# One fused kernel of two transformer blocks: high parts of split products first, the first loads on two queues, other step orders

## What is computed

```
layer 0: x = LN(a*x + mlstm(x))         mlstm: x @ w_in (3080 columns), 4 heads, gates, head norm, @ w_out
         x = LN(a*x + relu(x @ up)^2 @ down)      up: 1024 x 4096, down: 4096 x 1024
         x = x + sigmoid(x @ w_gate + b) * (p[0] @ w_proj)
layer 1: x = LN(a*x + attention with sinks and a window (x)), then the same two lines
block 2: h = h + 0.5 * (silu(n(h) @ wg) * (n(h) @ wu)) @ wd        n = rmsnorm, width 2816
         h = h + mixed(n(h)) @ w_out    mixed: compressed, selected and window attention, and one with forget gates
         h = h + 0.5 * swiglu again
         h = h + sigmoid(n(h) @ w_gate) * n(p @ w_proj)
```

## Time and profile before

| | |
|---|---|
| median of 3 runs | 1231.56 us (1231.07 to 1232.04) |
| profiled execution | 1232.38 us, its span 1230.7 us |
| TensorE (PE) busy | 1198.8 us, 97%, 5861 matmuls |
| weight loads (PEld) | 991.3 us, 81% |
| VectorE (DVE) | 745.4 us, 61% |
| ScalarE (ACT) | 618.3 us, 50% |
| GpSimd (POOL) | 43.2 us, 4% |
| memory traffic | 210.72 MB, mean 171 GB/s |

### The profile page before, as it was taken

How to read it: one execution, slowest core, us unless ns; L and a number is a source line. 1 busy time by engine, 2 the same in 40 slices (tenths; PEclk the granted TensorE clock), 3 DMA queues, 4 the chain that set the end, 5 groups by cost and what they waited for, 6 DMA issues and landing times.

```text
span 1230.7 us, 15102 instructions
## 1 busy us (share of the span) xinstructions
PE 1198.8 (97%) x5861; PEld 991.3 (81%) x5861; DVE 745.4 (61%) x983; ACT 618.3 (50%) x925; POOL 43.2 (4%) x61
## 2 busy tenths in 40 slices
PE   7999999999999989999999999999999999999998
PEld 6887788888788768888877888888878788888877
DVE  5648754545876585455587545447976465545456
ACT  4554434434465544434446444436886565444445
POOL 1000000000000000000000000000202010000001
PEclk9999999999999999999999999999999999999999
DMA  8546455465652454655545555564652327555550
GB/s 285 183 150 221 154 206 184 160 207 188 201 180 76 138 196 163 204 190 173 189 151 184 192 181 172 195 206 128 189 172 69 112 75 235 187 181 176 191 171 35
DMA packets 119959, 210.72 MB, mean 171 GB/s; under 512 B 8320, under 2 KB 67024, under 8 KB 119888
## 3 DMA queue, kind: packets, MB, share of 16 engines
q1 hardware_dynamic: 119888, 209.75, 51.5%
HBM read 208.68 MB, written 1.05 MB: 170 GB/s over the span
## 4 chain that ended last, share of the span: by engine, by line
PE 89%; DVE 7%; ACT 1%; issue 1%; DMA 1%; POOL 0%; SPq 0%; DVEq 0%; POOLq 0%; ACTq 0%
PE psum L341 26%; PE psum L343 26%; PE psum L342 26%; PE psum L1333 2%; PE psum L1365 2%; PE psum L480 2%; DVE wl L324 1%; PE psum L1352 1%; PE psum L787 1%; DVE xT_low L742 1%; DVE bn L709 1%; DMA ring<-in_a_w_in 1%; PE psum L1336 0%; DVE x L733 0%; ACT xT_high L765 0%
## 5 line engine op out<-in xcount | busy, mean ns | idle before, releaser
L293 DVE TENSOR_TENSOR wl<-ring,wh 128x2048 fp32r<-128x2048 f32 x131 | 300.0, 2292 | 270.5 <-ACT wh L284 270.5
L341 PE MATMUL psum<-wh,xT_high 128*128 128x512 f32 (+4 forms) x944 | 371.6, 394 | 3.3 <-DVE xT_low L3414 1.9
L343 PE MATMUL psum<-wh,xT_low 128*128 128x512 f32 (+4 forms) x944 | 362.8, 384 | 0.0
L342 PE MATMUL psum<-wl,xT_high 128*128 128x512 f32 (+4 forms) x944 | 362.0, 383 | 0.0
L284 ACT ACTIVATE wh<-ring 128x2048 fp32r<-128x2048 f32 x131 | 250.5, 1915 | 218.9 <-PE psum L343 218.9
L341 PEld LDWEIGHTS psum<-wh,xT_high 128*128 128x128 f32 x944 | 178.2, 189 | 36.6 <-DVE wl L324 2.3
L343 PEld LDWEIGHTS psum<-wh,xT_low 128*128 128x128 f32 x944 | 177.9, 188 | 34.9
L342 PEld LDWEIGHTS psum<-wl,xT_high 128*128 128x128 f32 x944 | 178.4, 189 | 31.1
L341 PE MATMUL psum<-wh,hidT_high 128*128 128x512 f32 (+1 forms) x520 | 199.5, 385 | 2.6 <-DVE hidT_low L3506 1.9
L343 PE MATMUL psum<-wh,hidT_low 128*128 128x512 f32 (+1 forms) x520 | 197.3, 381 | 0.0
L342 PE MATMUL psum<-wl,hidT_high 128*128 128x512 f32 (+1 forms) x520 | 197.2, 381 | 0.0
(11 more groups left out here) (289 smaller groups left out, 1080.0 us busy)
## 6 DMA issues: line engine op xcount, KB each, us to landing
ring<-in_mlp_w_up SPq DMA_DIRECT2D x32, 1024.0 KB, 5.3
ring<-in_mlp_w_down SPq DMA_DIRECT2D x32, 1024.0 KB, 4.9
ring<-in_ffn_wg SPq DMA_DIRECT2D x44, 512.0 KB, 4.0
ring<-in_ffn_wu SPq DMA_DIRECT2D x44, 512.0 KB, 5.0
ring<-in_ffn_wd SPq DMA_DIRECT2D x22, 1024.0 KB, 5.1
ring<-in_ple_w_gate SPq DMA_DIRECT2D x12, 1024.0 KB, 5.2
ring<-in_w_in SPq DMA_DIRECT2D x10, 1024.0 KB, 5.1
ring<-in_a_w_in SPq DMA_DIRECT2D x8, 1024.0 KB, 9.8
```

The source lines that it names most:

```text
L293: K.nc.vector.tensor_tensor(low[:, 0:w], K.ring[:, n % SLOTS, 0:w], high[:, 0:w].bitcast(F32), ALU.subtract).then_inc(K.low_ready, 2)
L341: nc.tensor.matmul(out, x[0], w[0], start=start, stop=False)
L342: nc.tensor.matmul(out, x[0], w[1], start=False, stop=False)
L343: return nc.tensor.matmul(out, x[1], w[0], start=False, stop=stop)
```

## The change

Five things are done.

1. `product` is taken apart into `product_high` (the two matmuls with x high) and `product_low` (the one with x low). `up_half_turned` makes a half of a product behind a turn: it waits for `high`, makes 8 matmuls, waits for `low`, makes 4. It is used for every `lead` and for t = 1 of the first product of each stage behind a tail (also in `dense` of the sink and the last mixer, written out there, and in `embed`). The waits are now per half, not for all four.
2. `step`, `piece` and `last` of the output products make the high matmuls first and wait for `z_low` in the middle; the wait ahead of them is for `z_high`.
3. `lead` of a feed-forward writes bank 0, and the readers of that bank follow through `up_bank`.
4. At the start the first half of load 0 is issued by ScalarE; SyncE issues the first half of `x`, the second half of load 0, the second half of `x`. The first `dense` steps take k = 0 and 1 and are placed before `xturn` 2 and 3, and they wait per pair for `input_high` and `input_low`.
5. The step lists of the first mixer, the sinks mixer and all nine tails are in another order.

```diff
+def product_high(K, out, x, w, start):
+    nc = K.nc
+    nc.tensor.matmul(out, x[0], w[0], start=start, stop=False)
+    nc.tensor.matmul(out, x[0], w[1], start=False, stop=False)
+
+def product_low(K, out, x, w, stop):
+    return K.nc.tensor.matmul(out, x[1], w[0], start=False, stop=stop)
...
+def up_half_turned(K, pe, where, gated, n, half, t, high, low):
...
+    pe.wait_ge(K.high_turned.sem, high)
+    for k in range(KT // 2):
+        if gated and k == 0 or not gated and k % 2 == 0:
+            weights_here(K, pe, n, 1 if gated else k // 2)
+        product_high(K, out, xs(k), [x[:, k, :, :] for x in w], half == 0 and k == 0)
+    pe.wait_ge(K.low_turned.sem, low)
+    for k in range(KT // 2):
+        mm = product_low(K, out, xs(k), [x[:, k, :, :] for x in w], half == 1 and k == KT // 2 - 1)
     return mm
...
+    up_bank = lambda c, t: 0 if led and c == 0 and t == 0 else 4 + t
...
-            if c == 0:
-                pe.wait_ge(K.low_turned.sem, x_low0)
...
+                if c == 0:
+                    mm = up_half_turned(K, pe, up_bank(c, t), gated, n, half, t, x_high0 - 1 + half, x_low0 - 1 + half)
...
             elif step == "lead":
                 half, = args
                 where, gated = self.lead
-                pe.wait_ge(K.low_turned.sem, self.low0 + half + 1)
                 if own and half == 0:
                     own("free")
-                mm = up_half(K, pe, where, gated, self.lead_load + half, half, 0)
+                mm = up_half_turned(K, pe, where, gated, self.lead_load + half, half, 0, self.high0 + half + 1,
+                                    self.low0 + half + 1)
...
-    def last(self, pe, load, t, h):
+    def last(self, pe, load, t, h, low=None):
...
+            product_high(K, K.psum[:, 2 * t + h, :], self.stat(2 * load + k, t), w[k], False)
+        if low:
+            pe.wait_ge(K.z_low.sem, low)
+        for k in range(2):
+            mm = product_low(K, K.psum[:, 2 * t + h, :], self.stat(2 * load + k, t), w[k], load == 3 and k == 1)
...
-        to_ffn, to_gated, to_rest = (4, False), (4, True), (0, False)
+        to_ffn, to_gated, to_rest = (0, False), (0, True), (0, False)
```

The start, in the first mixer's list, on SyncE and on ScalarE:

```diff
+        yield "xturn", 0
+        yield "xturn", 1
         yield "high", 0, 0
         yield "low", 0, 0
+        yield "dense", 0, 0, 0, range(2)
+        yield "dense", 0, 0, 1, range(2)
+        yield "high", 0, 1
         yield "low", 0, 1
-        yield "high", 0, 1
-        yield "xturn", 0
-        yield "xturn", 1
         yield "xturn", 2
         yield "xturn", 3
+        yield "dense", 0, 0, 0, range(2, 4)
+        yield "dense", 0, 0, 1, range(2, 4)
...
-        for half, x_sem, w_sem in ((0, K.input_loaded, K.first_loaded), (1, K.rest_loaded, K.slot_loaded[0])):
...
+        sp.dma_start(K.x[:, :, 0:BANK], x_rows[:, :, 0:BANK]).then_inc(K.input_loaded, 16)
+        for dst, src in zip(pieces_in(K, 0, K.ring[:, 0, :]), K.loads[0]):
+            sp.dma_start(dst[:, 2:4, :], src[:, 2:4, :]).then_inc(K.slot_loaded[0], 16)
+        sp.dma_start(K.x[:, :, BANK:D], x_rows[:, :, BANK:D]).then_inc(K.rest_loaded, 16)
...
+        for dst, src in zip(pieces_in(K, 0, K.ring[:, 0, :]), K.loads[0]):
+            act.dma_start(dst[:, 0:2, :], src[:, 0:2, :]).then_inc(K.first_loaded, 16)
```

More of the change, by code:

```diff
@@ L852, in after_mlstm @@
     yield "normal", 0, 1
+    yield "low", 0, 0
+    yield "last", 3, 1
     yield "turn", 0, 1
-    yield "last", 3, 1
     yield "lead", 0
@@ L1213, in after_ffn2 @@
     yield "emb", 1, 1
+    yield "copy", 0, 0
+    yield "square", 0, 1
+    yield "copy", 0, 1
+    yield "lead_high", 1, 1
     yield "high", 0, 1
[L1215 removed]
     yield "copy", 1, 0
     yield "copy", 1, 1
[L1218 to L1219 removed]
+    yield "high", 1, 0
     yield "lead_low", 1, 0
+    yield "low", 0, 1
+    yield "turn", 1, 0
+    yield "turn", 1, 1
+    yield "lead", 0
     yield "lead_low", 1, 1
[L1222 to L1224 removed]
     yield "low", 1, 0
     yield "low", 1, 1
[L1227 removed]
     yield "square", 1, 0
+    yield "high", 1, 1
     yield "square", 1, 1
[L1230 removed]
     yield "lead", 1
@@ L1626, in steps @@
         yield "high", 2, 0
-        yield "dense", 0, 0, 1, range(2)
+        yield "dense", 0, 0, 1, range(4)
         yield "high", 2, 1
         yield "low", 2, 0
-        yield "take", 0, 0
         yield "high", 3, 0
         yield "low", 2, 1
-        yield "dense", 0, 0, 1, range(2, 4)
-        yield "low", 3, 0
-        yield "high", 3, 1
         yield "dense", 0, 1, 1, range(2)
         yield "dense", 0, 1, 1, range(2, 4)
+        yield "take", 0, 0
         yield "take", 0, 1
+        yield "high", 3, 1
@@ L1639, in steps @@
         yield "high", 4, 0
         yield "rotate", 0
-        yield "low", 3, 1
         yield "dense", 1, 0, 0, range(2)
         yield "dense", 1, 0, 0, range(2, 4)
+        yield "high", 4, 1
+        yield "low", 3, 0
+        yield "dense", 1, 0, 1, range(2)
+        yield "tiles", 0
+        yield "dense", 1, 0, 1, range(2, 4)
+        yield "low", 3, 1
+        yield "tiles", 2
+        yield "tiles", 1
         yield "residual", 0
-        yield "dense", 1, 0, 1, range(2)
-        yield "high", 4, 1
+        yield "dense", 1, 1, 0, range(2)
@@ L1661, in steps @@
         yield "scores", 2
+        yield "low", 5, 0
+        yield "dense", 1, 1, 1, range(2, 4)
+        yield "high", 6, 0
+        yield "take", 1, 1
+        yield "scores", 3
         yield "turn", 0
-        yield "low", 5, 0
+        yield "dense", 2, 0, 0, range(2)
         yield "low", 5, 1
-        yield "dense", 1, 1, 1, range(2, 4)
-        yield "take", 1, 1
-        yield "dense", 2, 0, 0, range(2)
+        yield "dense", 2, 0, 0, range(2, 4)
+        yield "high", 6, 1
+        yield "rotate", 1
@@ L1683, in steps @@
-        yield "dense", 2, 0, 1, range(2, 4)
-        yield "low", 6, 0
-        yield "values", 2
-        yield "high", 7, 0
+        yield "turn", 3
+        yield "values", 2
+        yield "dense", 2, 0, 1, range(2, 4)
+        yield "high", 7, 0
+        yield "high", 7, 1
+        yield "low", 6, 0
+        yield "values", 3
+        yield "shares", 0
+        yield "dense", 2, 1, 0, range(2)
+        yield "group", 0
+        yield "low", 6, 1
         yield "scores", 5
-        yield "low", 6, 1
@@ L1689, in steps @@
-        yield "high", 7, 1
-        yield "values", 3
         yield "turn", 4
-        yield "group", 0
-        yield "dense", 2, 1, 0, range(2)
         yield "scores", 6
-        yield "turn", 5
-        yield "dense", 2, 1, 0, range(2, 4)
-        yield "take", 2, 0
-        yield "scores", 7
-        yield "sink", 1
         yield "low", 7, 0
         yield "low", 7, 1
+        yield "dense", 2, 1, 0, range(2, 4)
+        yield "turn", 5
+        yield "zturn", 0
+        yield "scores", 7
@@ L1731, in steps @@
         yield "scores", 11
-        yield "turn", 10
+        yield "low", 8, 1
         yield "values", 8
@@ L2617, in own @@
                 if load == 2 and h == 0:
-                    pe.wait_ge(K.z_low.sem, zl0 + 4)
-                out.last(pe, load, 1, h)
+                    pe.wait_ge(K.z_high.sem, zh0 + 4)
+                out.last(pe, load, 1, h, zl0 + 4)
         follow.pe(pe, own)
@@ L3012, in steps @@
         yield "take", 1, 1
+        yield "colturn",
+        yield "low", 5, 1
         yield "high", 6, 1
         yield "tiles", 0
+        yield "gcol",
         yield "tiles", 1
-        yield "gcol",
-        yield "take", 2, 0
-        yield "dense", 2, 1, 0, range(4)
-        yield "tiles", 2
-        yield "high", 7, 0
-        yield "high", 7, 1
-        yield "dense", 2, 1, 1, range(4)
+        yield "high", 7, 0
+        yield "low", 6, 0
+        yield "dense", 2, 1, 0, range(4)
+        yield "low", 6, 1
@@ L3023, in steps @@
+        yield "tiles", 2
+        yield "high", 7, 1
+        yield "angle",
+        yield "dense", 2, 1, 1, range(4)
+        yield "scores", 0
+        yield "take", 2, 0
+        yield "dense", 3, 0, 0, range(4)
+        yield "low", 7, 0
         yield "high", 8, 0
-        yield "low", 6, 1
-        yield "low", 7, 0
         yield "take", 2, 1
-        yield "angle",
-        yield "scores", 0
-        yield "dense", 3, 0, 0, range(4)
+        yield "low", 7, 1
+        yield "dense", 3, 0, 1, range(4)
@@ L3030, in steps @@
         yield "high", 8, 1
-        yield "dense", 3, 0, 1, range(4)
-        yield "low", 7, 1
+        yield "high", 9, 0
+        yield "low", 8, 0
         yield "tiles", 3
-        yield "high", 9, 0
+        yield "low", 8, 1
         yield "high", 9, 1
         yield "scores", 1
-        yield "low", 8, 0
+        yield "stats", 0
+        yield "dense", 3, 1, 0, range(4)
         yield "values", 0
-        yield "dense", 3, 1, 0, range(4)
-        yield "stats", 0
-        yield "low", 8, 1
+        yield "take", 3, 0
@@ L3071, in steps @@
+        yield "dense", 4, 0, 1, range(4)
+        yield "dense", 4, 1, 0, range(4)
```

(8 more changed lines are left out.)

438 lines of the change are left out of this document (224 added, 214 removed).

## The result

The changed kernel takes 1217.59 us (median of 4 runs, 1217.09 to 1219.56), the kernel before 1231.80 beside it: 14.2 us less, ratio 0.9888 (95% interval 0.9871 to 0.9905). The forecast was 1220.2 with a range of 1213.5 to 1228.

The account below looks back on a forecast made before the run. TensorE, busy 1198.8 of 1230.7 us, was taken to bound the kernel, so only its waits count. Terms 1.4 + 5.2 + 0.7 + 2.0 + 2.1 + 1.0 - 1.0 = 11.4 us gave 1220.2, range 1213.5 to 1228.

Parts of the forecast that it names:

- likeliest case: The summed forecast of 1220.2 us, alone spanning 1215.5 to 1224; chance 0.47.
- The start, 1.4: Kernel start: first product at 10.1 us, 2.7 earlier, less 1.3 for transposes now inside the stream; net 1.4 us.
- shared-engines rival: Start: with both queues at once x comes only at 7.0, gaining 0.1 us; 1221.5 us in all; chance 0.15.
- Low halves, 5.2 and 0.7: After turns, 8 high matmuls cover the wait for low: 5.2 us; same rule at the attention mixer's end: 0.7.
- The embedding copy: At `lead` behind the embedding, 0.7 us put down to `xT_low` is really ScalarE's last bank copy and stays.
- End of the first mixer, 2.0: `hidT_low` wait of 1.9 and clock loss of 1.6 go, 3.5 together, less a new `z` wait of 1.5.
- Step orders, 2.1: Waits for finished rows x before turns shrink after first mixer (1.1), first feed-forward (0.6) and sinks mixer (0.4).
- the softmax 1.0: The 1.0 us softmax wait goes because a piece of six matmuls (1.4) is placed ahead of that turn.
- a loss of 1.0: Inside the mixers: many further steps change place with unpriced new neighbours; 1.0 us lost, bounds nothing and 3.
- Slower, from 0.14 us a wait: About 80 added mid-product waits each expose a stationary load of 0.18 us, 14.4 in all; 1234.6 us; chance 0.07.
- The signs: Right if: first product 9.5 to 11.5, `xT_low` under 1.5, no 0.50 clock after start, softmax wait gone, copy wait 0.7.
- signs of "wrong": Waits on x as long, new `wl` waits inside mixers, idle tenths before low passes, or first product after 12 us.

Follow-up runs that it names:

- the start alone: Kernel before with only the changed loads and order of splits and first products at the start: 1232.61 us (12 runs), ratio 0.9995; undisturbed runs 1229.4 to 1231.1.
- orders alone: Kernel before with the changed step orders and changed start loads, its old products still waiting for low before any matmul: 1224.18 us, ratio 0.9926.
- the split alone: Changed kernel with old step orders in tails and both mixers and the old four start loads, keeping high matmuls before the low wait: 1224.21 us, ratio 0.9924.

## Why the prediction was right, point by point

**Direction, size, mechanism.** Right: forecast 11.4 us, measured 14.2 by the medians, 14.9 by the spans, inside the likeliest case's own range. Of the 3.5 us between forecast and spans, 1.0 is a loss that did not come, 1.3 is spread over the start and four other terms, and 1.2 lies in no wait that I can name.

**The start, 1.4.** Right in size: 1.9 at the 300th matmul of the profiled pair, 1.8 by the start alone in its undisturbed runs. Its steps were partly off. I took `x` at 5.8 and it came at 4.71; I took the first product at 10.1 and it began at 9.21; the transposes of the second half cost 1.05 in the stream (at most 1.3), and a wait of 0.45 on weights behind them was not foreseen. The shared-engines rival (first product 11.3) is wrong, and so is half of the reason that I gave for the gain: the order of the splits and products brought it, the second queue at most 0.6. The slow clock of the start moved along as forecast: matmuls of 392 columns follow one another at 0.33 us until 13.3 and at 0.18 from then on, 4.1 us behind the first product; before it was until 16.7, 3.9 behind it.

**Low halves, 5.2 and 0.7.** Right in size: no `xT_low` wait of a tail is left (6.3 became 0.69 for the copy and 0.20 for `xT_high`, so 5.4) and the 0.8 of the earlier trace rows is gone; orders alone against both together is 4.6 by the spans, 6.6 by the medians. What failed is the step that names the cause, so the size is luck in part: waits that vanish add up to the same sum whichever part of the edit takes them. I put the whole gain down to 8 matmuls made before the wait (1.8 us of cover). The runs give those 2.0 to 2.3; the larger part, 2.6 to 4.3, comes with the wait for each half by itself, so that a product no longer waits for the other half's low part. The place that I worked through showed it (high ended at 133.04, the product started at 134.47, two low passes of 0.7 later), and I read over it. "0.4 remains for `high` itself": 0.2 remained.

**The embedding copy.** Right: 0.69 stayed and is now named as the copy.

**End of the first mixer, 2.0.** Measured 2.3 to 2.4. The new wait on `z` was 0.93, not 1.5: I had counted to the end of VectorE's second `z` pass (92.12 in the trace after), and the turn needs only the first (91.52). The old wait of 1.92 and the clock's fall behind it went whole, but a wait of 0.34 on the embedding input behind it (105.04 us) is new, and I had none there: 3.5 - 0.93 - 0.34 is 2.2. Two sizes that were off in opposite directions make up much of the agreement. The split and the order were not both needed: the orders alone give all 2.4, the split alone 1.9.

**Step orders, 2.1, the softmax 1.0, and a loss of 1.0.** The first is right: the waits on `x` of the tails fell from 4.1 to 0.8 (3.3), and the new waits on `wl` behind the sinks mixer, which I had counted, take 0.97 of that back, so 2.3. The softmax wait went (its 1.0). The mis-sized term is the loss. New waits of 0.47 on `x` in the second embedding stage and 0.21 on `z` in the last mixer did come, but two waits that I had in no term went: 0.43 on `hidT_low` in the sinks mixer, and 0.23 on `x` in the last embedding. That leaves nothing of the -1.0. The sum as measured is 1.9 for the start, 5.4, 0.8, 2.3 for the mixer's end, 2.3, 1.0 and 0: 13.7, against 14.9. The other 1.2 is no wait but part of the 3.7 by which TensorE's busy time fell; its cause stays open.

**Slower, from 0.14 us a wait.** Wrong: the price is under a fortieth of that.

**The signs.** First product in 9.5 to 11.5: it was 9.21, outside on the good side. `xT_low` under 1.5: it is 0, part of it named `xT_high` (0.2). No stretch at 0.50 after the start: so in the profiled run; in 3 of 8 runs the mean clock is 0.997 or 0.998, so it can still happen. Of the signs of "wrong" one is there in small: a new wait on `wl` inside a mixer, the 0.45 at 16.91 us in the start of the first.

## What to carry to other kernels

When a consumer waits for several parts, count the passes between the part that it needs first and the one that it waits for: a wait for too much (both halves, all four copies) costs whole passes, and taking it apart costs nothing measurable, here a few lines for 3.7 us (2.8 by the spans). Before moving work into a gap, ask whether the engine that ends the wait has a gap itself; where VectorE ran without one, three orders moved the same wait from one name to the next. A measurement of the parts one by one is needed even when the sum comes out right, because two parts may cover the same wait and a third may be worth nothing by itself.

## What the hardware showed that I had not expected

A satisfied wait of TensorE between matmuls of one product: under 0.003 us. The granted clock can fall to its lower level behind waits of 1.1 and 1.4 us, or of 0.43 and 0.82, and was there for 3.4 to 6.8 us in the ten falls seen, in some executions of a program and not in others (kernel before: 20 of 39 runs at a mean of 0.997 or less). Two queues at the start did not delay the first load (4.71 against 4.67), and loads of the same program land at times that move the 300th matmul by up to 1.1 us.
